# Variances of the layer and group norms summed on four column groups and kept a quarter wide

## The chip, the cores and the metric

The kernel runs on one core of a Trainium2 chip. The metric is the device time of one execution in microseconds, the median over several runs.

## The reference, cut to what matters

A hybrid diffusion backbone of two layers over 256 context tokens and 256 latent tokens of width 1024. Each layer has an input projection, a bidirectional RWKV-7 scan over eight heads of 64 beside a gated short convolution, an output projection, a post-norm, a channel mixer (dense SwiGLU in layer 0, top-2-of-8 experts in layer 1) and a second post-norm. The two kinds of norm are what the change touches:

```
def layer_norm(x, g, b):                       # over the 1024 features of a token
    mu = mean(x, -1); var = mean(square(x - mu), -1)
    return (x - mu) * rsqrt(var + LN_EPS) * g + b

def rwkv_readout(y, terms, gd, r_k, g2, lnx_g, lnx_b):      # y: (tokens, 8 heads, 64)
    mu = mean(y, -1); var = mean(square(y - mu), -1)
    yn = (y - mu) * rsqrt(var + GN_EPS)
    bonus = sum over directions of sum(r * k * r_k, -1) * v
    out = yn * lnx_g + lnx_b + bonus
    return out * (sigmoid(gd) @ g2)
```

The context stream is dropped in the last layer, so the group norm of layer 1 and the layer norms in it run on 256 tokens and not on 512.

## The kernel before, in words

Everything is held with features on the 128 partitions and tokens on the columns: X is 8 blocks (KD) of 128 features by T = 512 tokens, Y is 4 blocks (NP) of two heads each. The work of each engine is one program, written out by hand, and the engines meet by semaphores. So each engine works through its list in order, and an instruction that waits holds up all behind it.

A layer norm (`ln_pe`, `ln_act`, `ln_dve`) goes so. TensorE multiplies the 8 blocks of X with `mean_w`, a 128x128 matrix of 1/1024, into bank 4 of PSUM: every partition of that bank then holds the mean of each token. VectorE subtracts it (L1513). ScalarE squares each block into one of two buffers SQ (L1213), and TensorE sums the squares in the same way into bank 5 (L1900), again with the same value on all 128 partitions. ScalarE may fill a buffer only when the matmul that read it is done. VectorE adds the epsilon (L1516), ScalarE takes the root (L1215), VectorE the reciprocal (L1518), all 128 partitions by 512 (or 256) tokens, then multiplies the 8 blocks (L1521). ScalarE applies gain and bias (L1218). There are four layer norms, numbered n = 0 to 3; the first two are on 512 tokens, the last two on 256.

The group norm stands between the scan and the output projection of each layer. With `heads`, a matrix of ones in two diagonal blocks of 64, TensorE sums each head of the four blocks of Y (L2174), VectorE centres (L1761), ScalarE squares (L1388), TensorE sums the squares of each block (L2179), and each block has its own add (L1765), root (L1392), reciprocal (L1769) and product (L1771). ScalarE then applies gain and bias to Y (L1395). TensorE has meanwhile made the gate (L2183) into four banks, and the bonus sums (L2189) into two banks that take turns, so that the third and fourth wait for the first and second result. VectorE multiplies the bonus with V (L1775), adds (L1777) and multiplies with the gate (L1779). ScalarE and GpSimd split each result into a high and a low half (L1400, L1154), and the output projection begins with the convolution's blocks and needs the low half of the last of the others to go on.

Weights are loaded by the SP queue into a ring, split into a high part by ScalarE (L309) and a low part by GpSimd (L315), and used in three matmuls (L325, L326, L327). One such split (the first unit of the output projection) stands in ScalarE's list between the squares and the roots of the group norm. Behind the third layer norm come the router and the experts, whose weights the SP queue begins to load into a ring of seven slots once the second output projection is done; it refills a slot when TensorE has used it (L523, L528).

## Time and profile before

| | us |
|---|---|
| median of 3 runs | 2465.11 (2463.06 to 2473.86) |
| profiled execution | 2466.55 |
| its span, first to last instruction | 2464.8 |
| TensorE matmuls busy in the span | 2233.3 (91%) |
| VectorE, ScalarE, GpSimd busy | 759.5, 627.7, 586.6 |

All times of the trace are in microseconds from the start of the span. A busy TensorE is not TensorE at its peak, since its matmuls are pipelined. A fp32 matmul shows as two records.

### The profile page before, as it was taken

To read this page: it belongs to the slowest core of one execution; us is meant where nothing else is said; L and a number is where in the kernel's file an instruction comes from. 1 tells how busy PE (TensorE), PEld (TensorE's weight loads), DVE (VectorE), ACT (ScalarE), POOL (GpSimd) and SP (SyncE) were. 2 spreads that over 40 slices of the span, in tenths; PEclk is the share of its full clock that TensorE was granted. 3 is DMA by queue.
4 is the path that set the end of the run, shared out by engine and by line. 5 is a ranking of instruction groups with operands and counts; after the bars stand their busy time and mean duration, and the time that the engine had idled before them with its cause. 6 is when DMAs were issued, how large, how long until landed. Compare 5 with 4: busy or idle time off the path is not lost.

```text
span 2464.8 us, 57159 instructions
## 1 busy us (share of the span) xinstructions
PE 2233.3 (91%) x26022; PEld 1430.8 (58%) x26022; DVE 759.5 (31%) x1354; ACT 627.7 (25%) x944; POOL 586.6 (24%) x386
## 2 busy tenths in 40 slices
PE   4999798797999999969869877999999999999995
PEld 2677577565787777848747667444444444343352
DVE  2227766634222222261585653100000000000002
ACT  1243554423222222232646542000000000000002
POOL 5233443241343343423454322000000000000000
PEclk9999899998999999989989988999999999999997
DMA  7543001226534435313100125999999999999993
GB/s 259 195 158 109 6 4 37 87 77 215 179 135 171 154 129 178 102 52 129 43 6 4 37 71 223 385 397 398 404 398 403 398 401 404 383 397 408 408 396 115
DMA packets 192781, 521.16 MB, mean 211 GB/s; under 512 B 7312, under 2 KB 82208, under 8 KB 186912
## 3 DMA queue, kind: packets, MB, share of 16 engines
q1 hardware_dynamic: 182288, 485.38, 52.5%
q10 hardware_dynamic: 9104, 27.97, 3.4%
q8 instruction: 205, 3.36, 0.6%
q0 software_dynamic: 1152, 4.19, 0.5%
q14 instruction: 32, 0.26, 0.0%
HBM read 496.15 MB, written 21.36 MB: 210 GB/s over the span
## 4 chain that ended last, share of the span: by engine, by line
PE 44%; issue 38%; DVE 9%; ACT 4%; DMA 2%; POOL 1%; ACTq 0%; POOLq 0%; DVEq 0%; SPq 0%
PE bank L325 9%; PE bank L327 9%; PE bank L326 9%; PE bank L2003 2%; PE bank L1999 2%; PE bank L2014 2%; PE bank L1880 1%; POOL w_lo L315 1%; PE bank L1976 1%; DVE arena L1541 1%; PE bank L1867 1%; PE bank L1896 1%; PE bank L1900 1%; DVE arena L1769 1%; ACT w_hi L309 1%
## 5 line engine op out<-in xcount | busy, mean ns | idle before, releaser
L315 POOL TENSOR_TENSOR w_lo<-arena,w_hi 128x2048 fp32r<-128x2048 f32 x78 | 354.3, 4543 | 623.5 <-ACT w_hi L309 623.5
L857 PE MATMUL bank<-arena 128*32 128x512 f32 (+1 forms) x3680 | 445.4, 556 | 0.6 <-ACT arena L609 0.6
L325 PE MATMUL bank<-h_hi,w_hi 128*128 128x512 f32 (+1 forms) x1008 | 391.5, 388 | 48.7 <-DVE h_lo L1486 42.6
L326 PE MATMUL bank<-h_lo,w_hi 128*128 128x512 f32 (+1 forms) x1008 | 375.9, 373 | 0.0
L327 PE MATMUL bank<-h_hi,w_lo 128*128 128x512 f32 (+1 forms) x1008 | 375.7, 373 | 0.0
L860 PE MATMUL bank<-arena 128*32 128x256 f32 (+1 forms) x3680 | 265.8, 360 | 0.0
L325 PEld LDWEIGHTS bank<-h_hi,w_hi 128*128 128x128 f32 x1008 | 193.8, 192 | 114.4 <-issue 62.4
L860 PEld LDWEIGHTS bank<-arena 128*32 128x32 f32 x3680 | 119.6, 110 | 241.0 <-issue 227.4
L931 PE MATMUL bank<-arena 128*32 128x512 f32 (+1 forms) x2208 | 221.3, 558 | 10.4 <-DMA arena<-in_moe_w_dram 4.7
L326 PEld LDWEIGHTS bank<-h_lo,w_hi 128*128 128x128 f32 x1008 | 194.7, 193 | 35.2 <-issue 5.2
L593 POOL DMA_INDIRECT arena<-slot_y,arena x4 | 3.8, 950 | 880.4 <-ACTq L683 879.5
L327 PEld LDWEIGHTS bank<-h_hi,w_lo 128*128 128x128 f32 x1008 | 194.2, 193 | 32.8
L309 ACT ACTIVATE w_hi<-arena 128x2048 fp32r<-128x2048 f32 x78 | 147.1, 1887 | 202.3 <-PE bank L327 166.0
L931 PEld LDWEIGHTS bank<-arena 128*32 128x32 f32 x2208 | 75.4, 111 | 146.6 <-issue 134.5
L857 PEld LDWEIGHTS bank<-arena 128*32 128x32 f32 x3680 | 116.0, 110 | 66.3 <-issue 2.7
L1143 POOL TENSOR_TENSOR arena<-arena,level_c 128x256 f32<-128x256 f32 x160 | 131.2, 859 | 0.0
L795 DVE TENSOR_TENSOR arena<-arena,bank 128x768 f32<-128x768 f32 (+2 forms) x25 | 17.4, 713 | 353.4 <-ACT arena L653 353.4
L1315 ACT ACTIVATE arena<-bank 128x512 f32<-128x512 f32 x160 | 94.2, 596 | 71.1 <-PE bank L2003 70.0
L653 ACT ACTIVATE arena<-bank 128x768 f32<-128x768 f32 (+2 forms) x25 | 14.9, 618 | 381.9 <-PE bank L860 381.8
L780 DVE TENSOR_TENSOR arena<-arena,bank 128x1536 f32<-128x1536 f32 (+3 forms) x16 | 17.4, 1088 | 297.3 <-ACT arena L629 204.8
L1804 DVE TENSOR_TENSOR arena<-arena,bank 128x512 f32<-128x512 f32 x104 | 71.5, 687 | 60.1 <-PE bank L327 59.9
L325 PE MATMUL bank<-g_hi,w_hi 128*128 128x512 f32 x224 | 88.2, 394 | 0.4 <-POOL w_lo L315 0.4
(286 smaller groups left out, 2807.8 us busy)
## 6 DMA issues: line engine op xcount, KB each, us to landing
arena<-in_moe_w_dram SPq DMA_DIRECT2D x168, 2048.0 KB, 12.7
arena<-in_w_mod_dram SPq DMA_DIRECT2D x48, 1024.0 KB, 5.0
arena<-in_ffn_w_dram SPq DMA_DIRECT2D x42, 1024.0 KB, 7.1
arena<-in_w_in_dram SPq DMA_DIRECT2D x26, 1024.0 KB, 6.5
arena<-in_w_out_dram SPq DMA_DIRECT2D x8, 1024.0 KB, 9.6
slot_x<-arena ACTq DMA_DIRECT2D x1, 5376.0 KB, 28.2
slot_y<-arena ACTq DMA_DIRECT2D x1, 5376.0 KB, 57.1
x_store<-arena ACTq DMA_DIRECT2D x2, 2048.0 KB, 6.5
```

What stands on the lines that cost most here:

```text
L309: act.activation(split_views(key)[0], slot_view(key), ACT.Copy).then_inc(sem("w_hi"), 1)
L315: pool.tensor_tensor(lo, slot_view(splits[i][0]), hi, ALU.subtract).then_inc(sem("w_lo"), 1)
L325: nc.tensor.matmul(out_, ah, bh, start=(first and i == 0), stop=False)
L326: nc.tensor.matmul(out_, ah, bl, start=False, stop=False)
L327: ins = nc.tensor.matmul(out_, al, bh, start=False, stop=(last and i == n - 1))
L857: mm(bank[b][64 * h + 32 * c:64 * h + 32 * c + 32, 0:n // 2], xa[:, 32 * c:32 * c + 32], w[:, n // 2 * h:n // 2 * (h + 1)], start=first, s ...
L860: ins = mm(bank[b + 1][blk(q), 0:n // 4], xb, w[:, n // 4 * q:n // 4 * (q + 1)], start=first, stop=last)
L931: ins = mm(bank[b][64 * h + 32 * c:64 * h + 32 * c + 32, 0:n // 2], x64[:, 32 * c:32 * c + 32], w[:, n // 2 * h:n // 2 * (h + 1)], start=f ...
L1143: nc.gpsimd.tensor_tensor(w["LM"][:, k], w["LC"], level_c[:, d, k, None].to_broadcast([P, 4, HS]), ALU.mult) \
L1315: act.activation(wk[q]["XT"], ps[:, 4 * q:4 * q + 2, 0:2 * P], ACT.Copy).then_inc(sem("act_xs"), 1)
L1804: nc.vector.tensor_tensor(FACC[:, m], FACC[:, m], src, ALU.add).then_inc(sem("ffn_acc"), 1)
L1999: mm_t(bank[b + p][:, P:2 * P], t_[:, 2 * p:2 * p + 2].rearrange("s e t -> s (e t)"), ident)
```

## The change

Three things are changed, in both kinds of norm. First, the squares are summed on a quarter of the token columns at a time, each quarter on its own 32 columns of the array, so that the variances of one token quarter stand on one group of 32 partitions: 128 columns wide (64 for 256 tokens). In the group norm the four blocks of heads are put side by side, so that all four share one bank. Second, add, root and reciprocal are then made on this form, once for each norm. Third, four matmuls, each on 32 rows of the array, spread each quarter back over all 128 partitions, into four banks, and the products read from these. The layer norm's variance is multiplied by 1024 so that the sum over 32 equal rows gives the reciprocal root; the group norm's spreading matrix `spread` holds 1/16 where a row and a column belong to the same head.

In the group norm the order changes as well: the bonus sums come ahead of the variances on TensorE, in four banks of their own, and the gate's matmuls behind them, in the same banks; the product of bonus and V comes ahead of the root on VectorE; the bias is added to the bonus by ScalarE, and the gain is applied in the same VectorE instruction that adds the bonus.

```
+        spread = sb("spread", [P, P])
...
-        RSTD = area(o_ln + 1024, T)
+        var_t = area(o_ln + 1024, T)
...
+        def quarter(tok, q):
+            n = (tok.stop - tok.start) // 4
+            return slice(tok.start + n * q, tok.start + n * q + n)
...
+            link(nc.gpsimd.memset(spread[:], 1.0 / 16))
+            of_head = same[:, 4, :].rearrange("p (q h n) -> p q h n", q=4, h=2)[:, :, :, 0]
+            for q in (1, 2, 3):
+                link(nc.gpsimd.tensor_tensor(of_head[:, 0], of_head[:, 0], of_head[:, q], ALU.add))
+            by_head = spread[:].rearrange("p (h n) -> p h n", h=2)
+            link(nc.gpsimd.tensor_tensor(by_head, by_head, of_head[:, 0].unsqueeze(2).to_broadcast([P, 2, HS]), ALU.mult))
...
-                act.activation(RSTD[:, tok], RSTD[:, tok], ACT.Sqrt).then_inc(sem("ln_std"), 1)
+                act.activation(var_t[:, 0:w], var_t[:, 0:w], ACT.Sqrt).then_inc(sem("ln_std"), 1)
...
                 split_hi(act, split_of[("out", l, 0)])
+                act.wait_ge(sem("gn_ve"), l + 1)
+                act.activation(var_t[:, 0:4 * w], var_t[:, 0:4 * w], ACT.Sqrt).then_inc(sem("gn_std"), 1)
                 for j in range(NP):
-                    act.wait_ge(sem("gn_ve"), NP * l + j + 1)
-                    act.activation(RRS[:, j, rtok], RRS[:, j, rtok], ACT.Sqrt).then_inc(sem("gn_std"), 1)
-                for j in range(NP):
-                    act.wait_ge(sem("gn_norm"), NP * l + j + 1)
-                    act.activation(Y[:, j, rtok], Y[:, j, rtok], ACT.Identity, bias=pcol(l, "lnxb", j),
-                                   scale=pcol(l, "lnxg", j)).then_inc(sem("gn_aff"), 1)
+                    act.wait_ge(sem("bonus"), NP * l + j + 1)
+                    act.activation(RTB[:, j, rtok], RTB[:, j, rtok], ACT.Identity, bias=pcol(l, "lnxb", j)) \
+                       .then_inc(sem("gn_aff"), 1)
...
-                nc.vector.tensor_scalar(RSTD[:, tok], bank[5][:, tok], LN_EPS, None, ALU.add).then_inc(sem("ln_ve"), 1)
+                nc.vector.tensor_scalar(var_t[:, 0:w], bank[5][:, 0:w], LN_EPS, 32.0 * 32.0, ALU.add, ALU.mult).then_inc(sem("ln_ve"), 1)
                 dve.wait_ge(sem("ln_std"), n + 1)
-                link(nc.vector.reciprocal(RSTD[:, tok], RSTD[:, tok]))
+                nc.vector.reciprocal(var_t[:, 0:w], var_t[:, 0:w]).then_inc(sem("ln_inv"), 1)
                 wait(dve, "ln_sq", KD * (n + 1))
+                dve.wait_ge(sem("ln_rstd"), n + 1)
                 for k in range(KD):
-                    nc.vector.tensor_tensor(X[:, k, tok], X[:, k, tok], RSTD[:, tok], ALU.mult).then_inc(sem("ln_norm"), 1)
+                    x_ = X[:, k, tok].rearrange("p (q n) -> p q n", q=4)
+                    nc.vector.tensor_tensor(x_, x_, ps[:, 4:8, 0:w], ALU.mult).then_inc(sem("ln_norm"), 1)
...
                 for j in range(NP):
-                    dve.wait_ge(sem("gn_vmm"), NP * l + j + 1)
-                    nc.vector.tensor_scalar(RRS[:, j, rtok], bank[2 + j % 2][:, rtok], 1.0 / HS, GN_EPS, ALU.mult, ALU.add) \
-                      .then_inc(sem("gn_ve"), 1)
+                    dve.wait_ge(sem("bonus_mm"), NP * l + j + 1)
+                    nc.vector.tensor_tensor(RTB[:, j, rtok], V[:, j, rtok], bank[4 + j][:, rtok], ALU.mult) \
+                      .then_inc(sem("bonus"), 1)
+                dve.wait_ge(sem("gn_vmm"), NP * (l + 1))
+                nc.vector.tensor_scalar(var_t[:, 0:4 * w], bank[2][:, 0:4 * w], 1.0 / HS, GN_EPS, ALU.mult, ALU.add) \
+                  .then_inc(sem("gn_ve"), 1)
+                dve.wait_ge(sem("gn_std"), l + 1)
+                nc.vector.reciprocal(var_t[:, 0:4 * w], var_t[:, 0:4 * w]).then_inc(sem("gn_inv"), 1)
+                dve.wait_ge(sem("gn_rstd"), l + 1)
                 for j in range(NP):
-                    dve.wait_ge(sem("gn_std"), NP * l + j + 1)
-                    link(nc.vector.reciprocal(RRS[:, j, rtok], RRS[:, j, rtok]))
-                    nc.vector.tensor_tensor(Y[:, j, rtok], Y[:, j, rtok], RRS[:, j, rtok], ALU.mult)
+                    y_ = Y[:, j, rtok].rearrange("p (q n) -> p q n", q=4)
+                    nc.vector.tensor_tensor(y_, y_, ps[:, 0:4, w * j:w * j + w], ALU.mult).then_inc(sem("gn_norm"), 1)
                 for j in range(NP):
-                    link(nc.vector.tensor_tensor(RTB[:, j, rtok], V[:, j, rtok], bank[4 + j % 2][:, rtok], ALU.mult))
-                    link(nc.vector.tensor_tensor(Y[:, j, rtok], Y[:, j, rtok], RTB[:, j, rtok], ALU.add))
-                    nc.vector.tensor_tensor(MIX[:, j, rtok], Y[:, j, rtok], bank[(6, 7, 0, 1)[j]][:, rtok], ALU.mult) \
+                    link(nc.vector.scalar_tensor_tensor(out=Y[:, j, rtok], in0=Y[:, j, rtok], scalar=pcol(l, "lnxg", j),
+                                                        in1=RTB[:, j, rtok], op0=ALU.mult, op1=ALU.add))
+                    nc.vector.tensor_tensor(MIX[:, j, rtok], Y[:, j, rtok], bank[4 + j][:, rtok], ALU.mult) \
                       .then_inc(sem("mix"), 1)
...
-                    mm(bank[5][:, tok], mean_w[:], SQ[:, k % 2, tok], start=(k == 0), stop=(k == KD - 1)) \
-                        .then_inc(sem("ln_vmm"), 1)
+                    for q in range(4):
+                        ins = mm(bank[5][blk(q), 0:w], mean_w[:, 0:32], SQ[:, k % 2, quarter(tok, q)], start=(k == 0),
+                                 stop=(k == KD - 1))
+                    ins.then_inc(sem("ln_vmm"), 1)
+                pe.wait_ge(sem("ln_inv"), n + 1)
+                for q in range(4):
+                    ins = mm(bank[4 + q][:, 0:w], ones_t[blk(q), :], var_t[blk(q), 0:w], start=True, stop=True)
+                ins.then_inc(sem("ln_rstd"), 1)
...
                 for j in range(NP):
+                    pe.wait_ge(sem("bonus_in"), NP * l + j + 1)
+                    mm(bank[4 + j][:, rtok], heads, RTB[:, j, rtok], start=True, stop=True).then_inc(sem("bonus_mm"), 1)
+                for j in range(NP):
                     pe.wait_ge(sem("gn_sq"), NP * l + j + 1)
-                    mm(bank[2 + j % 2][:, rtok], heads, RSQ[:, j, rtok], start=True, stop=True).then_inc(sem("gn_vmm"), 1)
+                    for q in range(4):
+                        ins = mm(bank[2][blk(q), w * j:w * j + w], keep[:, 1, 48:80], RSQ[:, j, quarter(rtok, q)], start=True,
+                                 stop=True)
+                    ins.then_inc(sem("gn_vmm"), 1)
                 pe.wait_ge(sem("g2_load"), 16 * (l + 1))
                 for j in range(NP):
-                    mm(bank[(6, 7, 0, 1)[j]][:, rtok], g2[:, j * P:(j + 1) * P], GD[:, rtok], start=True, stop=True) \
+                    pe.wait_ge(sem("bonus"), NP * l + j + 1)
+                    mm(bank[4 + j][:, rtok], g2[:, j * P:(j + 1) * P], GD[:, rtok], start=True, stop=True) \
                         .then_inc(sem("gate_mm"), 1)
-                for j in range(NP):
-                    mm(bank[4 + j % 2][:, rtok], heads, RTB[:, j, rtok], start=True, stop=True) \
-                        .then_inc(sem("bonus_mm"), 1)
+                pe.wait_ge(sem("gn_inv"), l + 1)
+                for q in range(4):
+                    ins = mm(bank[q][:, 0:4 * w], spread[blk(q), :], var_t[blk(q), 0:4 * w], start=True, stop=True)
+                ins.then_inc(sem("gn_rstd"), 1)
-                pe.wait_ge(sem("gn_ve"), NP * (l + 1))
+                pe.wait_ge(sem("gn_norm"), NP * (l + 1))
```

Here `w` is a quarter of the token count, `blk(q)` the partitions 32q to 32q + 31, and `rtok` the tokens of the layer.

## Rows read from the trace of the kernel before

**Rows 1.** The page, its first part: busy time, share of span, instructions.

```profile
PE 2233.3 (91%) x26022; PEld 1430.8 (58%) x26022; DVE 759.5 (31%) x1354; ACT 627.7 (25%) x944; POOL 586.6 (24%) x386
```

**Rows 2.** Timeline, group norm of layer 0: start, duration, engine, line, operation, [idle before].

```profile
473.45 0.69 DVE L1761 SCALAR_TENSOR_TENSOR arena<-bank,arena 128x512 f32<-128x512 f32 x1 [0.17 <-PE bank L2174]
...
478.58 3.35 DVE L1769 RECIPROCAL arena<-arena 128x512 f32<-128x512 f32 x1 [0.75 <-ACT arena L1392]
...
495.25 0.69 DVE L1777 TENSOR_TENSOR arena<-arena 128x512 f32<-128x512 f32 x1
...
495.98 0.69 DVE L1779 TENSOR_TENSOR arena<-arena,bank 128x512 f32<-128x512 f32 x1
...
503.35 0.69 DVE L1779 TENSOR_TENSOR arena<-arena,bank 128x512 f32<-128x512 f32 x1
...
504.78 1.29 POOL L1154 TENSOR_TENSOR h_lo<-arena,h_hi 128x512 fp32r<-128x512 f32 x1 [0.31 <-ACT h_hi L1400]
```

**Rows 3.** Timeline, group norm of layer 1, 256 tokens.

```profile
1463.79 1.34 ACT L1392 ACTIVATE arena<-arena 128x256 f32<-128x256 f32 x4
...
1474.07 0.42 DVE L1777 TENSOR_TENSOR arena<-arena 128x256 f32<-128x256 f32 x1
...
1474.53 0.42 DVE L1779 TENSOR_TENSOR arena<-arena,bank 128x256 f32<-128x256 f32 x1
...
1479.01 0.42 DVE L1779 TENSOR_TENSOR arena<-arena,bank 128x256 f32<-128x256 f32 x1
```

**Rows 4.** One line's instructions, layer norms: duration in ns as minimum/median/maximum.

```profile
L1516 DVE TENSOR_SCALAR arena<-bank x4: 426/558/692, 561.3 to 2450.2; 128x512 f32<-128x512 f32 x2, 128x256 f32<-128x256 f32 x2
...
L1518 DVE RECIPROCAL arena<-arena x4: 1752/2553/3353, 562.7 to 2451.2; 128x512 f32<-128x512 f32 x2, 128x256 f32<-128x256 f32 x2
...
L1215 ACT ACTIVATE arena<-arena x4: 416/523/629, 562.1 to 2450.7; 128x512 f32<-128x512 f32 x2, 128x256 f32<-128x256 f32 x2
```

**Rows 5.** Timeline, first layer norm, 512 tokens.

```profile
545.12 7.03 PE L1896 MATMUL bank<-arena,mean_w 128*128 128x512 f32 x16
...
552.91 1.23 ACT L1213 ACTIVATE arena<-arena 128x512 f32<-128x512 f32 x2 [5.62 <-DVE arena L1513]
...
559.49 0.63 ACT L1213 ACTIVATE arena<-arena 128x512 f32<-128x512 f32 x1 [0.23 <-PE bank L1900]
...
561.34 0.69 DVE L1516 TENSOR_SCALAR arena<-bank 128x512 f32<-128x512 f32 x1 [4.28 <-PE bank L1900]
...
566.11 4.91 DVE L1521 TENSOR_TENSOR arena<-arena 128x512 f32<-128x512 f32 x8
```

**Rows 6.** Timeline, second layer norm (first row) and third (256 tokens).

```profile
1091.00 1.28 ACT L1215 ACT_TABLE_LOAD   x1
...
1512.89 0.85 ACT L1213 ACTIVATE arena<-arena 128x256 f32<-128x256 f32 x2 [0.42 <-PE bank L1900]
...
1517.23 2.77 DVE L1521 TENSOR_TENSOR arena<-arena 128x256 f32<-128x256 f32 x8
```

**Rows 7.** Timeline, matmuls on small tiles in the experts and in the scan.

```profile
1542.97 1.04 PE L857 MATMUL bank<-arena 128*32 128x512 f32 x8
...
288.67 1.06 PE L1976 MATMUL bank<-arena 64*64 64x128 f32 x32
...
288.38 0.32 PEld L2003 LDWEIGHTS bank<-arena 64*64 64x64 f32 x16 [0.17 <-issue]
```

**Rows 8.** A stretch of the second group norm: busy times, then granted clock, DMA share, GB/s.

```profile
1462.00:1475.00 13.00, 0.51 (x3) 0.11 (x1) 10.55 (x12) 5.51 (x11) 4.50 (x1) 0.62 0.57 182
```

**Rows 9.** Chain of waits in the dense mixer; who waited in the experts (total, times, longest).

```profile
603.31 17.48 DMA arena<-in_ffn_w_dram
...
PE bank L931 <- DMA arena<-in_moe_w_dram: 4.7, 3, 3.1
...
SPq L523 <- PE bank L860: 472.6, 98, 22.0
```

**Rows 10.** Timeline, GpSimd's first weight split behind its constants.

```profile
52.03 9.01 POOL L315 TENSOR_TENSOR w_lo<-arena,w_hi 128x2048 fp32r<-128x2048 f32 x2 [23.47 <-ACT w_hi L309]
```

More of the change, by code:

```diff
@@ L1214, in ln_act @@
                 act.wait_ge(sem("ln_ve"), n + 1)
-                act.activation(RSTD[:, tok], RSTD[:, tok], ACT.Sqrt).then_inc(sem("ln_std"), 1)
+                w = (tok.stop - tok.start) // 4
+                act.activation(var_t[:, 0:w], var_t[:, 0:w], ACT.Sqrt).then_inc(sem("ln_std"), 1)
                 for k in range(KD):
@@ L1384, in _ @@
                 rtok = LTOK(l)
+                w = (rtok.stop - rtok.start) // 4
                 act.wait_ge(sem("y_done"), YTOT[l])
@@ L1897, in ln_pe @@
                 ins.then_inc(sem("ln_mean"), 1)
+                w = (tok.stop - tok.start) // 4
                 for k in range(KD):
                     pe.wait_ge(sem("ln_sq"), KD * n + k + 1)
[L1900 to L1901 removed]
+                    for q in range(4):
[6 more added lines that the diff above has]
+                ins.then_inc(sem("ln_rstd"), 1)
             mod_first()
@@ L2170, in _ @@
                 pe.wait_ge(sem("state_done"), UTOT[l])
+                w = (rtok.stop - rtok.start) // 4
                 for j in range(NP):
```

16 lines of the change are left out of this document (5 added, 11 removed).

## The prediction

> **What bounds the kernel now.** I read the page first. TensorE is busy for 91% of the span [rows 1], but that share mixes stages with different limits, and it says nothing about the places that the diff touches. So I read the timeline of each of the six norms: two group norms (one per layer) and four layer norms. In all six the reader sees the same picture. TensorE has nothing to do, and a chain of single instructions on VectorE and ScalarE sets when it starts again.
>
> In the first group norm VectorE centres the last of the four head pairs at 473.45, then makes four reciprocals of 3.35 us, each followed by a product, and ends with four groups of add and gate, of which the last starts at 503.35. GpSimd's last low half, which the output projection waits for, ends at 504.78 + 1.29 = 506.07 [rows 2]. In the second (256 tokens) the square roots start at 1463.79, behind a weight split and a table load that the change leaves alone, and the last gate product ends at 1479.01 + 0.42 = 1479.43 [rows 3]. In the first layer norm the eight squares begin at 552.91, the last ends at 559.49 + 0.63 = 560.12, the added epsilon starts at 561.34, and the first normalized column block is written from 566.11 on [rows 5]. Rows 4 give the three instructions of that tail at both widths, in one line each: minimum at 256 columns, maximum at 512.
>
> **Reciprocal, root and add.** Between 256 and 512 columns the reciprocal grows from 1.752 to 3.353 us, 6.25 ns a column with almost no fixed part; the root from 0.416 to 0.629, 0.83 ns a column; the add from 0.426 to 0.692, 1.04 ns a column [rows 4]. Laid along these lines, at 128 columns they cost 0.95, 0.31 and 0.29 us, and at 64 columns 0.55, 0.26 and 0.23 us. Those are the widths of the new layer norms, a quarter of 512 and of 256. The group norm keeps the full width, but for all four pairs at once: one reciprocal in place of four.
>
> **The products that sum and spread.** A full matmul of 512 columns in fp32 is two records, and 16 records take 7.03 us back to back, 0.43 us a record [rows 5]. Four column groups work at once: eight records of 128*32 with 512 columns take 1.04 us with their tail, for what would be 3.4 in a row [rows 7]. Row groups overlap too, as far as the trace shows it: 32 records of 64*64 with 128 columns take 1.06 us with their tail, where one after another they would take 32 x 0.107 = 3.4 [rows 7]. Since 64*64 has only two column groups, half of that factor comes from rows. Tiles of 32*128, which spread the result, are not in the trace. Bounds: four at once (the four quarters cost one) and none at once (they cost four). I take four at once, as the nearest rows show both kinds overlapping. So a quartet costs 0.86 us at 512 columns, 0.43 at 256, 0.21 at 128, 0.11 at 64. Handing over to TensorE, loading its weights and handing back cost 0.36 us: in rows 5 the last square ends at 560.12 and the add starts 1.22 later, of which 0.86 is the matmul.
>
> The Trainium skill (TensorE: Matmul & The Clock Gate, the table of matmul optimizations) gives 3.07 times for four tiles of K=32 at N=512, not 4. By it the spread of the first group norm would be an estimated 1.1 us and not 0.86, and the forecast under half a microsecond later. No row here has this tile.
>
> **First group norm.** Work is also moved here: the four bonus matmuls come ahead of the variances on TensorE, the gate matmuls behind them, and the products with V ahead of the root on VectorE. The last centring starts at 473.45, when its matmul is through. Behind it now stand four bonus matmuls (4 x 0.86) and four quartets of variances (4 x 0.21): 4.3 us, so the one add starts at 477.75. VectorE does the four products meanwhile. Add 0.69, root 0.63, reciprocal 3.35 and gaps: 482.5. The gate matmuls (3.4 us) run under these; the additions of the bias to the bonus on ScalarE run under the reciprocal. If that cover were gone, four gate matmuls would cost about 2 us, since they end 1.4 us ahead of the reciprocal. Spread 0.86 + 0.36: 483.7. Four products at 0.61 (eight take 4.91 [rows 5]; there from SBUF, here with PSUM, where the add from PSUM costs the same 0.69): 486.15. Then per pair one combined multiply-add and one gate product. Their pitch is 495.98 - 495.25 = 0.73 and 0.61, so three pairs at 1.34 and a last one at 0.73 + 0.69: 491.6. Before, it was 503.35 + 0.69 = 504.04. GpSimd's low halves follow closer now (1.3 to 1.7 us each against a pitch of 1.34), for which I give back 0.6. Gain 11.8 us.
>
> **Second group norm.** The root can't start before 1463.79, since split and table load stand ahead of it as before. Root 0.42, reciprocal 1.75: 1466.0. TensorE has been idle for some 4 us then, and in this stretch its granted clock averages 0.62, so it has fallen to the lower level, 1.2 GHz, for a good part of it [rows 8]. I charge the spread at that level, 0.86 + 0.5: 1467.4. Four products at 0.34: 1468.75. Three pairs at (1474.53 - 1474.07) + 0.34 = 0.80 and a last one of 0.46 + 0.42: 1472.0, against 1479.43. With 0.1 for GpSimd: 7.3 us.
>
> **Layer norms.** In the first, a square's successor no longer waits for a matmul of 0.86 us. ScalarE's own pitch is 0.62 (two in 1.23), VectorE delivers each 0.61, and I take 0.66: the last square ends at 558.2 and not 560.12. Add starts 0.36 + 0.21 later, 558.75; with 0.29, 0.31, 0.95 and gaps the reciprocal ends at 560.4; spread 0.57: 560.95, against 566.11. Gain 5.1 us. The second is alike, but its square root needs a table that is loaded right behind the last square, at 1091.00 for 1.28 us [rows 6]. That was hidden under a tail of 1.9 us. The new tail to the root is 0.86, so the load shows with 0.44: 4.7 us. In the third (256 tokens) the pairs of squares shorten by 0.32 at three handovers: the last ends at 1512.75 and not 1513.74; then 0.47 + 0.23 + 0.26 + 0.55 + 0.47 and gaps give 1514.8 against 1517.23 [rows 6]: 2.4 us. The fourth is alike and has the table load again, which shows with 1.30 - (0.47 + 0.23 + 0.03), less the 0.1 that showed before: 1.9 us.
>
> **Edits at nothing.** The constant for spreading adds five GpSimd instructions of at most 128 columns at the start. GpSimd waits 23.47 us for ScalarE right behind its constants [rows 10], and nobody asks for them sooner; without this cover they would cost at most 5 x 1.29 us, the price of one of 512 columns [rows 2].
>
> **Does what follows move along?** After each norm all starts by semaphore. Even the long transfer on the path, 17.48 us at 603.31 [rows 9], is asked for by TensorE's progress and slowed by the zero writes that ScalarE issues right after the first layer norm; both move together. The experts' stage is the doubtful one: TensorE never waits there until the last third, then 4.7 us in 3 waits, and SP's queue waits for TensorE for 472.6 us [rows 9]. TensorE leads, so an earlier start passes through.
>
> **Sum.** 11.8 + 7.3 + 5.1 + 4.7 + 2.4 + 1.9 = 33.2 us. The profiled execution took 2466.55 us (span 2464.8 and 1.75 around it): 2433.35. It lies 1.44 above the median of 2465.11, so I forecast 2432.
>
> **Rivals.**
> *The small tiles don't overlap (8%).* Spreading one after another costs 2.6 + 2.6 + 2 x 0.64 + 2 x 0.32 = 7.1 us: 2439. If the variance quartets did not either, the layer norms' loops would stay as they are (7.6) and the first group norm lose 2.6: 2449. Against it: rows 7.
> *Changing the tile form costs (8%).* The change adds 3 changes of form in each layer norm and 4 in each group norm, 20 in all. In the scan, where forms alternate, the weight loads show a gap of 0.17 us at one [rows 7]. At that price on all 20: 3.4 us, 2435.5. The Trainium skill (TensorEngine Tiling (Array Packing), Key Properties) says that changing the tiling mode drains the TensorE, which speaks against this change; rows 7 have such a gap, and it is small. This is also the case on the other side: it makes the kernel slower than before by over 0.5% if a change of form costs (33.2 + 12.3) / 20 = 2.3 us, for which the scan with its many changes has no room (2%).
> *The experts' weights decide (8%).* SP's longest wait there is 22.0 us, while the first seven units fill the ring [rows 9]. If the transfers, and not TensorE, set the end of that stage, the third layer norm's 2.4 us are lost: 2434.5.
> *The forecast:* 74%.
>
> **Range.** From all overlaps perfect, no charge for the clock, GpSimd or table (some 4 us) and a run-to-run spread of 0.2%: 2424. Upward to tiles without overlap and a few microseconds: 2443. A measurement of this kernel can tell about 0.5% (12.3 us). All rivals but the slow one and half of the serial tiles lie over that: faster 0.95, same 0.03, slower 0.02.
>
> **What would show it.** One reciprocal of 3.35 us in the first group norm, one of 1.75 in the second, of about 0.95 and 0.55 in the layer norms; the add of the first group norm some 4.3 us behind the last centring; from the end of a reciprocal to the first product about 0.6 us in a layer norm and 1.2 in the first group norm; squares at a pitch near 0.66; a table load that reaches the root in the second and fourth layer norm. It would be wrong if the quartets take several times their share, if the products from four banks of PSUM cost more than 0.61 at 512 columns, if the bonus and gate matmuls end behind the reciprocal, or if the experts' stage grows by what the norms gave.

## Result and the profile after

The changed kernel took 2440.05 us, the median of 4 runs (2437.9 to 2443.15), beside 2467.12 us for the kernel before on the same chip. The ratio is 0.9881, with a 95% interval of [0.9868, 0.9895]. The forecast of 2432 was 8 us too low; its range (2424 to 2443) holds the time. Two of the 8 us are the starting point: the forecast was laid from a median of 2465.11, and the four runs beside the changed kernel have 2467.12. The other six are gain: 33.2 us were forecast, 27.1 is the difference of the medians (the interval of the ratio allows 26 to 33). The profiled execution took 2440.95 us with a span of 2438.8, 26.0 less than the span before. The page hardly shows it. This is the line that answers to [rows 1]:

```profile
PE 2233.8 (92%) x26310; PEld 1434.9 (59%) x26310; DVE 730.2 (30%) x1342; ACT 622.5 (26%) x938; POOL 585.6 (24%) x391
```

TensorE is as busy as before and has 288 instructions more. What shrank is the time in which it had nothing to do. Here is the timeline of the changed kernel over the first group norm (VectorE with TensorE's last three groups), the answer to [rows 2]. Columns: start, duration, engine, line, operation, out<-in, count, and the idle time before with its releaser.

```profile
475.66 0.69 DVE L1777 SCALAR_TENSOR_TENSOR arena<-bank,arena 128x512 f32<-128x512 f32 x1 [0.17 <-PE bank L2203]
...
478.99 1.08 PE L2210 MATMUL bank<-arena,keep 128*32 128x128 f32 x32
480.00 3.70 PE L2216 MATMUL bank<-arena 128*128 128x512 f32 x8
480.13 0.69 DVE L1785 TENSOR_SCALAR arena<-bank 128x512 f32<-128x512 f32 x1 [0.35 <-PE bank L2210]
481.52 3.35 DVE L1788 RECIPROCAL arena<-arena 128x512 f32<-128x512 f32 x1 [0.69 <-ACT arena L1405]
484.93 1.14 PE L2220 MATMUL bank<-arena,spread 32*128 32x512 f32 x8 [1.23 <-DVE arena L1788]
486.21 2.48 DVE L1793 TENSOR_TENSOR arena<-arena,bank 128x512 f32<-128x512 f32 x4 [1.33 <-PE bank L2220]
...
489.99 0.74 DVE L1797 SCALAR_TENSOR_TENSOR arena<-arena,par 128x512 f32<-128x512 f32 x1
...
491.38 1.26 DVE L1797 SCALAR_TENSOR_TENSOR arena<-arena,par 128x512 f32<-128x512 f32 x1
...
493.28 1.05 DVE L1797 SCALAR_TENSOR_TENSOR arena<-arena,par 128x512 f32<-128x512 f32 x1
...
495.80 1.29 POOL L1166 TENSOR_TENSOR h_lo<-arena,h_hi 128x512 fp32r<-128x512 f32 x1 [0.31 <-ACT h_hi L1413]
```

One reciprocal stands where four were. The add (L1785) starts 4.47 us behind the last centring (forecast 4.3). The gate's matmuls (L2216) end at 483.70, ahead of the reciprocal's end at 484.87. From the last centring to the end of the last low half it is 21.43 us, against 32.62 in [rows 2]: 11.2 saved. The odd rows are the multiply-adds L1797: 0.74 for the second, but 1.26 and 1.05 for the last two.

The first layer norm of the changed kernel, timeline, to be laid beside [rows 5]:

```profile
543.12 4.87 DVE L1526 TENSOR_TENSOR arena<-arena,bank 128x512 f32<-128x512 f32 x8 [5.99 <-PE bank L1917]
...
548.01 1.23 ACT L1225 ACTIVATE arena<-arena 128x512 f32<-128x512 f32 x2 [0.24 <-DVE arena L1526]
...
550.02 0.29 DVE L1530 TENSOR_SCALAR arena<-bank 128x128 f32<-128x128 f32 x1 [2.02 <-PE bank L1923]
550.34 0.31 ACT L1228 ACTIVATE arena<-arena 128x128 f32<-128x128 f32 x1 [1.10 <-DVE arena L1530]
550.68 0.95 DVE L1532 RECIPROCAL arena<-arena 128x128 f32<-128x128 f32 x1 [0.38 <-ACT arena L1228]
551.69 0.81 PE L1928 MATMUL bank<-arena,keep 32*128 32x128 f32 x8 [1.74 <-DVE arena L1532]
552.64 3.68 DVE L1537 TENSOR_TENSOR arena<-arena,bank 128x512 f32<-128x512 f32 x6 [1.00 <-PE bank L1928]
```

Add, root and reciprocal cost what the straight line through two widths gave (0.29, 0.31, 0.95 us). The spread costs more: 1.00 us of waiting between reciprocal and product, where 0.57 was forecast.

The second layer norm shows the table load ahead of the root, as forecast from [rows 6]; ScalarE's timeline of the changed kernel:

```profile
1076.50 1.28 ACT L1228 ACT_TABLE_LOAD   x1
1077.79 0.31 ACT L1228 ACTIVATE arena<-arena 128x128 f32<-128x128 f32 x1
```

The second group norm, timeline of SP, ScalarE, GpSimd and VectorE of the changed kernel, beside [rows 3]:

```profile
1436.40 7.22 SPq L1067 DMA_DIRECT2D arena<-in_w_out_dram  x4
...
1443.59 1.91 ACT L310 ACTIVATE w_hi<-arena 128x2048 fp32r<-128x2048 f32 x1 [2.64 <-DMA arena<-in_w_out_dram]
1445.52 1.28 ACT L1405 ACT_TABLE_LOAD   x1
1445.58 4.50 POOL L316 TENSOR_TENSOR w_lo<-arena,w_hi 128x2048 fp32r<-128x2048 f32 x1 [14.86 <-ACT w_hi L310]
1446.81 0.42 ACT L1405 ACTIVATE arena<-arena 128x256 f32<-128x256 f32 x1
1447.26 1.75 DVE L1788 RECIPROCAL arena<-arena 128x256 f32<-128x256 f32 x1 [4.34 <-ACT arena L1405]
...
1451.78 0.48 DVE L1797 SCALAR_TENSOR_TENSOR arena<-arena,par 128x256 f32<-128x256 f32 x1
```

From the root to the last low half (1456.85) it is 10.04 us, against 16.91 before: 6.9 saved, 7.3 forecast. But look at what stands ahead of the root. The weight's split waits for its transfer, which took 7.22 us here, and 5.18 in the kernel before:

```profile
1455.37 5.18 SPq L1061 DMA_DIRECT2D arena<-in_w_out_dram  x4
```

And look at TensorE's clock in the output projection that follows. Windows of the kernel before and then of the changed kernel; the granted clock is the third value from the right:

```profile
1479.40:1484.00 4.60, 4.48 (x38) 4.28 (x36) 0.52 (x2) 2.22 (x2) 3.15 (x3) 1.00 0.00 0
```

```profile
1455.60:1460.00 4.40, 4.40 (x31) 4.04 (x31) 0.48 (x1) 2.22 (x2) 3.20 (x3) 0.82 0.00 0
```

In this execution of the kernel before, the projection ran at full clock to its end; in this one of the changed kernel it has 0.82 at its start and 0.93 in its last 17.8 us. Together the transfer and the clock give back some 3.5 us: from the scan's last VectorE instruction to the projection's last it was 50.2 us and is 46.8, a gain of 3.4 and not 6.9. The low clock in the projection doesn't come from the change: `const_only`, which has the old norm, shows 0.92, 0.80 and 0.96 in three windows of it, and 51.7 us for the same stretch.

### The profile page after: what moved, and what is told of

The parts are those of the page before. It is cut to its first block, busy times and chain, and to the rows that moved or that the text cites. A ratio compares the mean times of both kernels' runs of the same rounds, so it can differ in the third digit from the quotient of the medians.

```text
span 2438.8 us, 57708 instructions
## 1 busy us (share of the span) xinstructions
PE 2233.8 (92%) x26310; PEld 1434.9 (59%) x26310; DVE 730.2 (30%) x1342; ACT 622.5 (26%) x938; POOL 585.6 (24%) x391
## 4 chain that ended last, share of the span: by engine, by line
PE 45%; issue 38%; DVE 9%; ACT 4%; DMA 2%; POOL 1%; ACTq 0%; POOLq 0%; DVEq 0%; SPq 0%
PE bank L326 9%; PE bank L328 9%; PE bank L327 9%; PE bank L2031 2%; PE bank L2027 2%; PE bank L2042 2%; PE bank L1901 1%; DVE arena L1557 1%; PE bank L2004 1%; PE bank L1888 1%; POOL w_lo L316 1%; PE bank L1917 1%; PE bank L2013 1%; DVE arena L1511 1%; DMA arena<-in_ffn_w_dram 1%
```

## The experiments

**One kind of norm at a time.** `gn_only` has the group norms changed and the layer norms as before, `ln_only` the reverse, and `const_only` adds nothing but the five GpSimd instructions that make the spreading matrix. `after_again` is the changed kernel once more.

```
gn_only:     ln_* functions of before, group norm of after
ln_only:     ln_* functions of after, group norm of before
const_only:  before + the memset and four tensor_tensor of spread
```

> Only the two group norms are changed (with their new order); the four layer norms are as before. If the gain is the shortened chains, it is the two group norms' share: 11.2 and 4.9 to 6.9 us were read between landmarks of the changed kernel's trace, so some 16 to 18 us below the kernel before, about 2450, ratio 0.9930. If the whole saving came from the layer norms and the group norms only moved waits, no difference beyond 3 us. In the trace the first layer norm's square loop should keep the granted clock at 1.00, since its matmuls are full again.

> Only the four layer norms are changed. Between landmarks they gave 4.4 + 4.4 + 2.2 + 2.2 = 13.2 us: about 2454, ratio 0.9946. If the group norms and layer norms depend on each other (an overlap that only both together give), the gains of this and of the group norms alone don't add up to the 28 us of the whole change. The clock should fall to 0.50 inside the square loop of the layer norms on 512 tokens, as in the changed kernel.

> The kernel before with only the five GpSimd instructions added that make the spreading matrix, which nothing reads. The changed kernel was 1.2 us late at the first modulation matmul and 2.2 us late at the first group norm. If these instructions cost that, this kernel is 1 to 2.8 us slower than before and shows the first modulation matmul at about 27.9 where before has 26.7. If it is scatter between executions, no such shift: the interval covers 1 and the matmul starts within 0.5 us of before in some profiles and not in others.

> The changed kernel once more, for a second profile. What belongs to the kernel comes again to a tenth of a microsecond (the six norms between their landmarks); what is scatter does not: the late first weight of the second output projection (7.2 us against 5.2), the start that was 1.2 us late, the second layer norm's mean sums at half clock (8.23 against 7.11 us).

Measured, against 2468.07 us for the kernel before: `gn_only` 2447.75 us (ratio 0.9909, [0.989, 0.9929]), `ln_only` 2456.68 (0.9952, [0.9934, 0.9969]), `const_only` 2468.12 (0.9996, [0.9984, 1.0007]), `after_again` 2444.04 in its single run. By the ratios the two parts give 22.5 and 11.8 us, and 29.4 (0.9881) together; the forecast had 19.1 and 14.1, both within the intervals, and the difference between 34.3 and 29.4 lies within them as well. The constant costs nothing that can be measured, and the first modulation matmul starts at 27.0 (26.7 before), not at 27.9. In the square loop of the first layer norm the clock is 1.00 in `gn_only` and 0.85 in `ln_only`, as expected.

In the traces most norms are as long in the kernel that has them alone as in the whole one: the first group norm with its projection takes 61.0 us from the last centring in both (72.3 before), the second layer norm 10.2 us from the first subtraction to the first gain in both (14.6 before). Two stages vary from execution to execution. The second group norm with its projection takes 46.8 us in the changed kernel, 43.9 in `after_again` and 44.9 in `gn_only`. The first layer norm takes 9.5 us from the first subtraction to the first product, 8.9 in `after_again` and 9.3 in `ln_only`. Between their landmarks `after_again` repeats five of the six norms to a tenth of a microsecond, all but this one. The late transfer came in part (5.83 us), and the long mean sums of the second layer norm, taken for scatter, came again (14.3 us up to the first subtraction, 14.1 in the changed kernel). Nothing here shows that the parts disturb each other.

**Is it the order or the single reciprocal?** `reorder_only` has the new order of the group norm (bonus first, bias on ScalarE, gain in the multiply-add), but four adds, roots and reciprocals of full width and no spreading.

```
 for j in range(NP):
+    wait bonus_mm; RTB = V * bank[4 + j]      # ahead of the adds
 ...                                           # add, root, reciprocal, product for each j, as before
-    Y = Y * gain + bias (ScalarE);  Y = Y + RTB
+    RTB = RTB + bias (ScalarE);     Y = Y * gain + RTB
```

> The group norms with the new order alone (bonus sums ahead in four banks, product with V ahead, bias on the bonus, gain in the adding instruction, gate behind), but with the four full-width adds, roots, reciprocals and products of before; layer norms as before. If the one reciprocal is what pays, three of 3.35 and three of 1.75 us are still there: from the last centring to the last result of the second group norm and first projection only 1 to 4 us go, of the 11.2 and some 6 of the whole group norm change, so 2465 or so, ratio 0.998 to 1.000. If the order pays (the turns of bonus and result in two banks were the cost), this kernel has most of the group norm's 20 us.

Measured 2464.83 us against 2470.57 (ratio 0.9977, [0.9967, 0.9987]). Timeline of VectorE in its first group norm:

```profile
480.70 3.34 DVE L1787 RECIPROCAL arena<-arena 128x512 f32<-128x512 f32 x1
...
492.66 3.34 DVE L1787 RECIPROCAL arena<-arena 128x512 f32<-128x512 f32 x1
```

The four reciprocals hold VectorE from 480.70 to 496.00. This norm with its projection took 71.7 us from the last centring, 72.3 before; in the second, it took 13.7 us from the root to the end of the last gate and not 15.6. So in these traces the order alone is worth 0.6 and 2.0 us, and the change of form the rest of the 11.2 and 6.9. The ratio gives the order 5.7 us (3.2 to 8.2); what it has beyond 2.6 us these stretches don't show. It is far from the 22.5 us of `gn_only` in any case.

**Does a low clock make the spread slow?** In the changed kernel the sums of the squares keep TensorE less busy than before, and its granted clock is lower in them and behind them. Windows of the kernel before, then of the changed kernel: in each the squares of the first layer norm and its tail. The granted clock is the third value from the right.

```profile
552.00:560.00 8.00, 6.56 (x15) 2.16 (x14) 4.87 (x8) 4.89 (x8) 0.00 (x0) 1.00 0.40 132
560.00:566.00 6.00, 1.30 (x4) 0.30 (x2) 3.97 (x2) 0.75 (x2) 0.00 (x0) 0.83 0.00 0
...
543.00:550.00 7.00, 4.70 (x65) 1.52 (x64) 4.87 (x8) 4.92 (x8) 0.00 (x0) 0.70 0.46 153
550.00:553.00 3.00, 0.81 (x8) 0.52 (x8) 1.60 (x3) 0.31 (x1) 0.00 (x0) 0.50 0.00 0
```

`ln_warm` gives TensorE something to do in the layer norms, into a bank that nobody reads.

```
 behind each quartet that sums squares:
+    mm(bank[7][:, 0:P], mean_w[:], ones_t, start=True, stop=True)
 ahead of the wait for the reciprocal:
+    for _ in range(3): mm(bank[7][:, 0:2 * P], mean_w[:], <256 columns>, start=True, stop=True)
```

> The changed kernel with idle-time matmuls of constants in the layer norms: one of 128 columns behind each variance quartet and three of 256 columns behind the last, into a bank that the spread overwrites later. If the fall of the granted clock to 0.50 inside the square loop is why the spread took 1.0 us and not 0.57 (0.90 and not 0.47 on 256 tokens), the clock stays at 1.00 there and the gap from reciprocal to first product is 0.55 to 0.65 us on 512 tokens and 0.45 to 0.5 on 256; in all 1 to 2 us, near what three rounds can tell. If the gap is a fixed cost of 32-row tiles (a change of form, weight loads), it stays at 1.0 and 0.9 with the clock at 1.00.

Measured 2444.37 us (ratio 0.9896, [0.9874, 0.9917]), no gain. VectorE's timeline in the first and then in the second layer norm of `ln_warm`, and a window of each:

```profile
547.41 0.95 DVE L1532 RECIPROCAL arena<-arena 128x128 f32<-128x128 f32 x1 [0.38 <-ACT arena L1228]
549.06 2.48 DVE L1537 TENSOR_TENSOR arena<-arena,bank 128x512 f32<-128x512 f32 x4 [0.70 <-PE bank L1931]
...
1081.32 3.08 DVE L1537 TENSOR_TENSOR arena<-arena,bank 128x512 f32<-128x512 f32 x5 [2.23 <-PE bank L1931]
```

```profile
547.00:550.00 3.00, 1.90 (x15) 1.20 (x14) 1.93 (x4) 0.52 (x2) 0.00 (x0) 1.00 0.00 0
1070.00:1077.00 7.00, 7.00 (x60) 3.88 (x60) 2.24 (x4) 4.43 (x6) 0.00 (x0) 0.54 0.00 0
```

At full clock the wait for the spread is 0.70 us and not 1.00, so the clock makes 0.3 of the 0.43 by which the forecast was short. `psum_bias`, a kernel further down whose layer norms are those of the changed kernel, confirms it with no added matmul: in its execution the clock stayed at 1.00 until behind the spread of the first layer norm. A window of it, and VectorE's row:

```profile
543.50:547.10 3.60, 1.35 (x24) 0.63 (x24) 1.25 (x3) 1.04 (x3) 0.00 (x0) 1.00 0.01 2
...
547.09 1.28 DVE L1537 TENSOR_TENSOR arena<-arena,bank 128x512 f32<-128x512 f32 x2 [0.70 <-PE bank L1929]
```

So when exactly the clock falls is not fixed by the kernel.

In the second layer norm of `ln_warm` the clock was 1.00 as the squares began (at 1068.1), fell to 0.50 at 1070.5 in spite of the added work and stayed there for 10 us. Now the added matmuls themselves stood in the way: TensorE was busy for all 7 us of the window, and the wait became 2.23 us. That layer norm took 14.6 us instead of 10.2, as long as before the change. In the third and fourth (256 tokens) the clock held at 1.00, but the waits were 1.07 and 0.87 us where 0.45 to 0.5 was expected: the three added matmuls were still running when the reciprocal ended. These two took 8.15 us each from the first subtraction to the first product, 6.38 and 7.05 in the changed kernel. What the clock alone costs on 256 tokens no run here shows.

**What does one quartet cost?** `spread_twice` makes every spread twice.

```
     for q in range(4): ins = mm(bank[4 + q][:, 0:w], ones_t[blk(q), :], var_t[blk(q), 0:w], ...)
+    for q in range(4): ins = mm(bank[4 + q][:, 0:w], ones_t[blk(q), :], var_t[blk(q), 0:w], ...)
```

> The changed kernel with each spread made twice, the second with the same result. It prices a quartet of tiles of 32 rows by itself, with the hand-over left out. At a raised clock and with full overlap a quartet costs 0.86, 0.43, 0.21 and 0.11 us at 512, 256, 128 and 64 columns. If the 1.01 us from the end of the reciprocal to the first product in the first layer norm are a fixed cost of a change of tile form, the second quartet adds only its columns, 0.21 us. If the half clock makes them, it adds 0.43 us (128 columns at 1.2 GHz), and in the first group norm, where the clock is up, 0.86 us.

A single run took 2442.08 us. Timeline of TensorE and VectorE in the first group norm, and VectorE's rows in the first and the third layer norm:

```profile
484.79 1.04 PE L2224 MATMUL bank<-arena,spread 32*128 32x512 f32 x8
485.96 1.28 DVE L1793 TENSOR_TENSOR arena<-arena,bank 128x512 f32<-128x512 f32 x2 [2.19 <-PE bank L2224]
...
552.75 1.88 DVE L1537 TENSOR_TENSOR arena<-arena,bank 128x512 f32<-128x512 f32 x3 [1.43 <-PE bank L1930]
...
1491.86 2.40 DVE L1537 TENSOR_TENSOR arena<-arena,bank 128x256 f32<-128x256 f32 x7 [1.32 <-PE bank L1930]
```

The wait grew from 1.33 to 2.19 us in the first group norm: 0.86 for a quartet of 512 columns, to the hundredth what one full matmul costs, so tiles on four row groups overlap fully. In the second group norm (256 columns at clock 0.50) it grew from 1.43 to 2.28, and in the first layer norm (128 columns, 0.50) from 1.00 to 1.43: the columns at half clock give 0.86 and 0.43. In the third layer norm (64 columns, 0.50) it grew from 0.90 to 1.32, again 0.42, where columns alone give 0.21. So at half clock a quartet of 64 columns costs no less than one of 128, and for 128 columns it can't be told whether the columns or something else sets the 0.43. The eight weight loads of such a quartet took 0.52 us in the changed kernel, which makes them a likely cause; that is argued, not shown.

**A weight split behind the root.** In the second group norm the root stands behind a weight's split. `split_late` puts the root first.

```
-                split_hi(act, split_of[("out", l, 0)])
                 act.wait_ge(sem("gn_ve"), l + 1)
                 act.activation(var_t[:, 0:4 * w], var_t[:, 0:4 * w], ACT.Sqrt).then_inc(sem("gn_std"), 1)
+                split_hi(act, split_of[("out", l, 0)])
```

> The changed kernel, with ScalarE's split of the first output unit put behind the root of the group norm instead of ahead of it. In the changed kernel VectorE waits 4.3 us for the root of the second group norm, which stands behind a weight that lands late, its split (1.9) and a table load (1.3). If that order is now the bound there, the second group norm shortens by about 3.5 us (root at some 7 us behind the last scan result, not 9.5 to 11) and the first one stays: about 3.5 us below the changed kernel, ratio to before 0.9866 or so. If the weight's low half is next in line right away (GpSimd ends it when the projection would start), under 1 us is gained.

Measured 2438.6 us (ratio 0.9872, [0.9856, 0.9888]); the changed kernel has 0.9881, so 2.2 us of the expected 3.5, which the intervals don't separate from nothing. The root came 6.6 us behind the scan and not 10.5, but the last gate only 2.2 us sooner behind the scan (17.0 and 19.2): the first multiply-add took 2.65 us. So it was run again, beside a kernel that aims at this row.

> The changed kernel with the weight split behind the root of the group norm, once more and beside the next two, so that they are compared on one chip. Its first trace showed the root of the second group norm some 4 us sooner after the scan, but the first multiply-add behind the norm took 2.65 us instead of 0.48, and it ended when GpSimd's 4.5 us low half of the weight had ended. Theory A, a VectorE instruction with two operands in SBUF is held while GpSimd reads SBUF: the 2.65 us come again, and the ratio stays near 0.987. Theory B, it was chance: 0.48 us there, and the last gate 2 us sooner.

`psum_bias` is `split_late`, and in layer 1 the biased bonus goes to the unused half of the gate's bank, so that the multiply-add reads one operand from SBUF and one from PSUM.

```
-  act.wait_ge(sem("bonus"), NP * l + j + 1)
-  act.activation(RTB[:, j, rtok], RTB[:, j, rtok], ACT.Identity, bias=pcol(l, "lnxb", j))
+  act.wait_ge(sem("bonus" if l == 0 else "gate_mm"), NP * l + j + 1)
+  act.activation(RTB[:, j, rtok] if l == 0 else bank[4 + j][:, 0:256], RTB[:, j, rtok], ACT.Identity, ...)
...
-  in1=RTB[:, j, rtok]
+  in1=RTB[:, j, rtok] if l == 0 else bank[4 + j][:, 0:256]
```

> The kernel before it, and in layer 1 the biased bonus lies in the free half of the gate's bank in PSUM, so that the multiply-add has one operand in SBUF and one in PSUM. Theory A, two SBUF operands are what GpSimd holds up: the first multiply-add starts while GpSimd's 4.5 us low half runs and takes under 0.6 us, and the last gate product comes 2.0 to 2.2 us sooner behind the reciprocal (from 9.5 to some 7.4 us). The products of the output projection that need nothing of it run at half clock there, so perhaps 1 us of it reaches the next stage. Theory B, the operand has nothing to do with it: 2.65 us as before.

Measured on one chip, against 2469.24 us: `split_late_timed` 2436.1 us (0.9871, [0.9856, 0.9886]), `psum_bias` 2430.58 (0.985, [0.9836, 0.9863]). VectorE and GpSimd in the second group norm, timeline of `split_late_timed`:

```profile
1438.89 1.75 DVE L1788 RECIPROCAL arena<-arena 128x256 f32<-128x256 f32 x1 [0.48 <-ACT arena L1404]
1441.55 1.41 DVE L1793 TENSOR_TENSOR arena<-arena,bank 128x256 f32<-128x256 f32 x4 [0.91 <-PE bank L2220]
1442.88 3.64 DVE L1797 SCALAR_TENSOR_TENSOR arena<-arena,par 128x256 f32<-128x256 f32 x1
...
1441.72 4.51 POOL L316 TENSOR_TENSOR w_lo<-arena,w_hi 128x2048 fp32r<-128x2048 f32 x1 [14.21 <-ACT w_hi L310]
```

and the same rows of `psum_bias`:

```profile
1436.16 1.75 DVE L1788 RECIPROCAL arena<-arena 128x256 f32<-128x256 f32 x1 [0.48 <-ACT arena L1404]
...
1440.15 0.47 DVE L1797 SCALAR_TENSOR_TENSOR arena<-arena,par,bank 128x256 f32<-128x256 f32 x1
...
1438.60 4.53 POOL L316 TENSOR_TENSOR w_lo<-arena,w_hi 128x2048 fp32r<-128x2048 f32 x1 [13.81 <-ACT w_hi L310]
```

In the first kernel the multiply-add ends at 1446.52, 0.29 us behind GpSimd's low half of the weight (1446.23); the products ahead of it, which read PSUM, run freely beside the same GpSimd instruction. In the second the multiply-add reads PSUM, starts in the midst of GpSimd's instruction, and takes 0.47. So it is the second operand in SBUF that is held: theory A. From the reciprocal's start to the end of the last gate it is now 7.46 us, against 10.95, and from the scan's last VectorE instruction to the projection's last 40.1, against 44.3. The expectation of a gain of 2.0 to 2.2 us was made from the 2.65 of the first trace; this time the multiply-add had to wait 3.64. The intervals of the two ratios overlap a little, but the traces place 4.2 of the 6.7 us between the two spans in this stretch, 3.5 of them ahead of the last gate's end, and 0.5 in the first layer norm, which in `psum_bias` ran at full clock. `psum_bias` is the fastest kernel of this study.

**The table load ahead of the squares.** `hoist` is `split_late` with a root of one column ahead of the squares where a table load stood in the tail.

```
+                if n % 2:
+                    act.activation(csig[:, 0:1], csig[:, 0:1], ACT.Sqrt)
                 for k in range(KD): ...       # squares
```

> The first kernel of this call, and in the second and fourth layer norm a root of one column stands ahead of the squares, so that the table load of 1.28 us comes off the tail. The changed kernel loads it behind the last square and the root waits for it. By the forecast's step the load shows with 0.44 us in the second layer norm and with 0.54 in the fourth: those two get shorter by these amounts (10.2 to 9.8, 7.5 to 7.0), if the load ahead of the squares is hidden. The rival: squaring needs the other table, so that the load comes twice and each of the two grows by 1.3 us. The total changes by 1 us either way, which no timing tells.

Measured 2435.02 us (0.9866, [0.9851, 0.9881]) beside 2436.1 for `split_late_timed`. Its second layer norm took 10.0 us and not 10.2, where 9.8 was expected, its fourth 7.0 and not 7.5. ScalarE in the second:

```profile
1072.51 1.25 ACT L1227 ACTIVATE arena<-arena 128x512 f32<-128x512 f32 x2 [0.21 <-PE bank L1925]
1074.87 0.31 ACT L1230 ACTIVATE arena<-arena 128x128 f32<-128x128 f32 x1 [1.10 <-DVE arena L1532]
```

The table load is gone from between the two, and squaring doesn't bring the other table back. The root still starts 1.11 us behind the last square, because it now waits for the add. `best` joined this, `split_late` and the added matmuls of `ln_warm`:

> The late split and the idle-time matmuls together, and in the second and fourth layer norm a one-column root ahead of the squares, so that the table is there before it is wanted. Sum of the parts: 3.5 + 1.5 + 0.4 + 0.5, about 6 us below the changed kernel, ratio to before 0.9855 to 0.9865. If the parts only move the wait to the next instruction, the gain is that of the late split alone.

It took 2442.45 us (0.9894, [0.9878, 0.991]): none of the expected 6 us came, and it was no better than the changed kernel. Its third layer norm took 11.5 us where the changed kernel's took 6.8: there the products waited 2.48 us for the spread, with the three added matmuls ahead of it.

## Why the prediction was nearly right

Step by step, forecast and trace of the changed kernel:

| | forecast | measured | counted |
|---|---|---|---|
| first group norm | 11.8 | 11.2 | last centring to end of last low half |
| second group norm | 7.3 | 6.9 | root to end of last low half |
| first layer norm | 5.1 | 4.4 | first subtraction to first product |
| second | 4.7 | 4.4 | the same, 13.92 to 9.49 |
| third | 2.4 | 2.2 | the same, 8.59 to 6.38 |
| fourth | 1.9 | 1.6 | the same, 8.65 to 7.05 |
| sum | 33.2 | 30.7 | |

The mechanism was forecast as it came: the chains of the six norms shorten, one reciprocal stands for four, and what follows moves along. The sum was too large by terms named below; each of them is small.

**Right.** The straight lines for reciprocal, root and add over the width; the overlap of tiles on row groups, which was taken from tiles of 64*64; products from four banks of PSUM at 0.61 us each; the table load, at its size; the constant at nothing; the passing of the third layer norm's gain through the experts' stage, which took 874.6 us against 872.8, within what it scatters between the fourteen kernels (872.7 to 875.4).

**The rivals.** That the small tiles don't overlap is refuted by 0.86 us for a second quartet. The Trainium skill (TensorE: Matmul & The Clock Gate, Measured speedup vs the span model) gives 3.07 times for four row tiles of K=32 at 512 columns. A lone quartet here took 1.14 us for 3.44 in a row, which agrees with it, but the second one behind it added 0.86, which is 4.0 times. That changes of tile form cost: between L2210 and L2216 in the first group norm the form changes from 128*32 to 128*128, and the next matmul starts (480.00) before the modelled end of the last one (480.07). No gap shows there. At the spreads TensorE is idle beforehand, so whatever a change of form costs there lies within the waits above. The experts' weights did not decide: their stage is as long as before.

**Mis-sized: the spread in the layer norms.** The forecast charged 0.21 us (128 columns) plus 0.36 for the hand-over. The wait was 1.00 us: TensorE had fallen to half its clock while the squares were summed (0.50 in the tail), which `ln_warm` prices at 0.3 us. The forecast charged the lower clock in the second group norm alone. The same holds for the time from the last square to the add, 0.78 instead of 0.57. These two terms make 0.64 of the 0.7 us missing in the first layer norm. In `psum_bias`, where the clock stayed up, they measured 0.70 and 0.55, and the same norm took 8.52 us from the first subtraction to the first product, 5.4 less than before: at full clock the 5.1 us of the forecast were there.

**Mis-sized: VectorE against GpSimd in the first group norm.** The forecast gave 0.6 us back because GpSimd's low halves follow closer. They don't: from the last gate's end to the last low half's it is 2.03 us in both kernels. The real cost sits elsewhere: L1797 reads two operands in SBUF and stretches from 0.74 to 1.26 and 1.05 while a low half runs, 0.83 us in all, on VectorE's own chain. The add (4.47 us behind the last centring, not 4.3) and the spread's wait (1.33 instead of 1.22) add 0.3.

**The least firm step: that the second group norm's gain passes on in full.** The forecast had the root wait for the same split and table load as before, at the same time, and what follows at the same speed. In the profiled execution 3.4 passed on: the root waits for a weight's split, which waits for a transfer that took 7.22 us instead of 5.18, and the projection ran at a lower clock and needed some 1.5 us more. Neither is firm from one execution to the next, and the second hits the old norm too (`const_only`). The same transfer took 5.83 us in `after_again`, where 6.2 us passed on, and 5.30 in `gn_only`, with 5.3 passed on. The whole stretch from the scan's last VectorE instruction to the projection's took 50.2, 51.7 and 50.2 us in the three kernels with the old norm and the old order (before, `const_only`, `ln_only`) and 46.8, 43.9, 44.9 and 44.6 in four with the new one (the changed kernel, `after_again`, `gn_only`, `ln_warm`). Between the means lie 5.6 us: most of the 6.9 passes on, and the profiled execution of the changed kernel is the least favourable one. Over the ten kernels with the new group norm the transfer took 5.29 to 7.22 us, in the four without it 5.15 to 5.22 (before, `const_only`, `ln_only`, `reorder_only`). So the new norm seems to have a hand in it, and not by its order alone, which `reorder_only` has too; by what means stays open.

**The rest.** The spans differ by 26.0 us. With 3.4 in place of 6.9 the norms give 27.2. The others are stages that the change doesn't touch and that differ between executions: the second scan was 3.7 us shorter, the start 2.6 us later. The first scan took 202.8 to 207.5 us over the fourteen kernels, the second 186.3 to 191.4, in both kinds of kernel alike. The mean sums of the second layer norm took 14.1 us up to the first subtraction in the changed kernel and 13.0 in the kernel before, with the clock at 0.62 in one window of them and at 0.79 in the one before. `split_late`, with the new norm, had 13.0, and `reorder_only`, with the old one, 13.9, so this isn't the change's either.

## What to carry to other kernels

A reciprocal costs by the column, so bring a value that stands equally on many partitions to as few columns as the array can spread again, and do all of them at once: the spread costs one matmul's columns, not four (down to 128 columns, as far as was measured). Count on half the clock behind a stretch in which TensorE mostly waits, and don't fill it with idle matmuls that stand ahead of those it waits for. And where VectorE and GpSimd work at the same time on the path that sets the end, keep one operand of VectorE's instruction in PSUM.

## What the runs showed of the hardware that was not expected

- **A VectorE instruction with two operands in SBUF waits for GpSimd's whole instruction.** 0.48 us became 2.65 and 3.64, ending some 0.3 us behind the end of GpSimd's low half; with one operand in PSUM it took 0.47 beside the same instruction. The kernel before has it too. Its trace has 24 VectorE instructions (TENSOR_TENSOR and SCALAR_TENSOR_TENSOR) with no operand in PSUM that start beside a GpSimd TENSOR_TENSOR of over 0.6 us and would by themselves end ahead of it: every one ends 0.27 to 0.55 us behind it. Of 126 with an operand in PSUM in the same position none is stretched by more than 0.03 us. A reciprocal, which has one operand, isn't held either (1464.24, 1.75 us). These are its rows in the second group norm; the product's end, 1467.34, is 0.28 behind GpSimd's, and 0.9 us were lost there:

```profile
1466.03 1.31 DVE L1771 TENSOR_TENSOR arena<-arena 128x256 f32<-128x256 f32 x1
...
1462.56 4.50 POOL L315 TENSOR_TENSOR w_lo<-arena,w_hi 128x2048 fp32r<-128x2048 f32 x1 [12.86 <-ACT w_hi L309]
```

  The Trainium skill (SBUF — State Buffer, SBUF: two separate sides) says it: the ports that the two engines share are an exclusive lock, for a VectorE operation with two SBUF inputs against a GpSimd operation that reads SBUF, and the loser blocks for the whole instruction. These rows agree with it.
- **Making a loop lighter for TensorE can slow what follows it.** With a quarter of the columns in the sums, the granted clock of the first layer norm went from 1.00 before to 0.70 in the loop and from 0.83 to 0.50 behind it. The moment of the fall varies: 545.8 in the changed kernel, in the loop; 550.1 in `after_again`, behind its last square; 547.4 in `psum_bias`, behind the spread.
- **A second quartet of tiles on four row groups adds 0.86 us for 512 columns at full clock and 0.43 for 128 at half clock, but 0.42 for 64 too.** At half clock 64 columns gained nothing over 128.
